# Second layer's mixer: PSUM banks split five and three instead of six and two

## The reference

```python
proj = xn @ cd_w_in[j]
lru_x, lru_g, m_x, m_o, m_if = split_cols(proj, CD_SIZES)      # 512, 512, 512, 512, 8
y_a = rglru_group(lru_x, lru_g, ...)   # recurrent unit
y_b = mlstm_group(m_x, m_o, m_if, ...) # four heads of 128
mixed = jnp.concatenate([y_a, y_b], axis=-1)
h = h + mixed @ w_mix_out[layer]
```

## Time and profile before

| | |
|---|---|
| median of 3 runs | 3127.95 us (3123.73 to 3131.43) |
| profiled execution | 3129.56 us, of which the span of the trace 3127.8 us |
| TensorE busy | 3019.6 us, 97% |
| VectorE, ScalarE, GpSimd busy | 1737.6, 1273.0, 319.1 us |
| mixer of the second layer | from 1049.7 us (first x matmul) to 1254 us (end of out7) |

### The profile page before, as it was taken

How to read it: one execution, slowest core, us unless ns; L and a number is a source line. 1 busy time by engine, 2 the same in 40 slices (tenths; PEclk the granted TensorE clock), 3 DMA queues, 4 the chain that set the end, 5 groups by cost and what they waited for, 6 DMA issues and landing times.

```text
span 3127.8 us, 41482 instructions
## 1 busy us (share of the span) xinstructions
PE 3019.6 (97%) x17696; PEld 2470.8 (79%) x17696; DVE 1737.6 (56%) x2154; ACT 1273.0 (41%) x1702; POOL 319.1 (10%) x285
## 2 busy tenths in 40 slices
PE   8989889999999999999999998999999999999999
PEld 5877778777888766777888775689998888878998
DVE  6444454646544675546544755676666453566665
ACT  5433333433322564433322545544444333344442
POOL 1010001000000100000000200124221000013240
PEclk9999999999999999999999999999999999999999
DMA  5341023223332311323332231233332223233331
GB/s 184 111 112 29 29 73 125 98 78 81 96 91 86 113 57 54 108 68 92 97 88 89 88 86 36 54 91 102 100 114 91 85 85 97 69 87 102 100 106 65
DMA packets 340104, 274.89 MB, mean 88 GB/s; under 512 B 28768, under 2 KB 308832, under 8 KB 339408
## 3 DMA queue, kind: packets, MB, share of 16 engines
q1 hardware_dynamic: 335552, 252.83, 27.2%
q0 software_dynamic: 4368, 19.41, 1.8%
HBM read 263.83 MB, written 8.39 MB: 87 GB/s over the span
## 4 chain that ended last, share of the span: by engine, by line
PE 86%; DVE 7%; ACT 5%; issue 1%; POOL 0%; DMA 0%; DVEq 0%; SPq 0%; ACTq 0%; POOLq 0%
PE ps L189 85%; ACT arena L203 2%; DVE arena L220 2%; ACT whi L206 2%; DVE arena L212 1%; DVE wlo L212 1%; PE ps L192 1%; DVE hT L212 1%; DVE xlo L212 0%; ACT L203 0%; POOL arena L212 0%; DVE sml L229 0%; ACT arena L206 0%; DVE xlo L220 0%; DVE split L212 0%
## 5 line engine op out<-in xcount | busy, mean ns | idle before, releaser
L189 PE MATMUL ps<-split,whi 128*128 128x512 f32 (+1 forms) x3008 | 900.9, 377 | 14.5 <-DVE split L212 6.1
L212 DVE TENSOR_TENSOR wlo<-wraw,whi 128x2048 fp32r<-128x2048 f32 (+5 forms) x261 | 562.3, 2157 | 486.1 <-ACT whi L206 485.8
L189 PE MATMUL ps<-xhi,whi 128*128 128x512 f32 (+2 forms) x2040 | 766.7, 381 | 25.5 <-DVE wlo L212 10.1
L189 PE MATMUL ps<-xhi,wlo 128*128 128x512 f32 (+2 forms) x1984 | 743.7, 375 | 0.0
L189 PE MATMUL ps<-xlo,whi 128*128 128x512 f32 (+2 forms) x1944 | 731.1, 376 | 0.0
L189 PEld LDWEIGHTS ps<-split,whi 128*128 128x128 f32 x3008 | 548.3, 188 | 142.7 <-issue 24.9
L206 ACT ACTIVATE whi<-wraw 128x2048 fp32r<-128x2048 f32 (+5 forms) x261 | 457.2, 1755 | 347.6 <-PE ps L189 243.3
L189 PE MATMUL ps<-split,wlo 128*128 128x512 f32 (+1 forms) x1504 | 559.1, 372 | 0.0
L189 PEld LDWEIGHTS ps<-xhi,whi 128*128 128x128 f32 (+1 forms) x2040 | 382.2, 189 | 109.9 <-issue 14.4
L189 PEld LDWEIGHTS ps<-xhi,wlo 128*128 128x128 f32 (+1 forms) x1984 | 374.9, 189 | 69.5 <-issue 5.1
L189 PEld LDWEIGHTS ps<-xlo,whi 128*128 128x128 f32 (+1 forms) x1944 | 366.7, 189 | 68.9
(11 more groups left out here) (132 smaller groups left out, 2428.2 us busy)
## 6 DMA issues: line engine op xcount, KB each, us to landing
wraw<-in_ffn_w_up SPq DMA_DIRECT2D x128, 512.0 KB, 5.2
wraw<-in_odd_w_in SPq DMA_DIRECT2D x24, 1024.0 KB, 5.1
wraw<-in_ffn_w_gate SPq DMA_DIRECT2D x44, 512.0 KB, 4.0
wraw<-in_ffn_w_down SPq DMA_DIRECT2D x20, 1024.0 KB, 5.1
wraw<-in_ffn_w_down SPq DMA_DIRECT2D x24, 768.0 KB, 4.5
wraw<-in_xattn_wkv SPq DMA_DIRECT2D x16, 1024.0 KB, 5.6
wraw<-in_xattn_wq SPq DMA_DIRECT2D x8, 1024.0 KB, 5.2
wraw<-in_xattn_wo SPq DMA_DIRECT2D x8, 1024.0 KB, 5.2
```

Source lines behind the costliest of these rows:

```text
L189: return self.e.matmul(out, lhsT, rhs, start=start, stop=stop, skip_group_check=True)
L212: return self.e.tensor_tensor(out, a, b, op)
```

## The change

The tuple for the heads and gates becomes five banks and the one for the dense blocks three:

```diff
@@ -2596,7 +2596,7 @@
             o_lru = add_units("lru_out", [P] * 4, Wo[0:512, :])
             o_ml = add_units("out", [P] * 4, Wo[512:1024, :])
-            of, of_dense = (0, 1, 2, 3, 4, 5), (6, 7)
+            of, of_dense = (0, 1, 2, 3, 4), (5, 6, 7)
 
             def tensor(pe):
```

## The result

The changed kernel takes 3142.3 us (median of 6 runs, 3136.11 to 3145.43) against 3127.37 us for the kernel before in the same runs: ratio 1.0043, 95% interval 1.0033 to 1.0053, that is 13.4 us more (10.3 to 16.6); the two medians by themselves differ by 14.9. The forecast was 10.9 us more, 3138.9, in a range of 3132 to 3146. So the direction and the range are right, and the median is 3.4 us above the forecast. The profiled execution took 3144.8 us, its span 3143.0.

The account below looks back on a forecast made before the run. TensorE, busy 97% of the span, was taken to bound the kernel. The terms 1.95 + 1.0 + 5.15 + 2.1 + 0 + 0.7 gave 10.9 us more, 3138.9 us from a median of 3127.95, range 3132 to 3146.

Parts of the forecast that it names:

- Step 1: At i2, which takes r0's bank: TensorE waits 1.95 us for r0's Sigmoid, and ScalarE's chain moves too.
- D: Delay of ScalarE's chain from i2's wait and the clock behind it: 3.0 us, between 1.95 and 3.65.
- The clock behind it: Behind i2's wait: work lost to a slow TensorE clock, 1.0 us taken between 0 and 1.7.
- Step 2: At g2: its 4.23 us wait and slow clock go, but s0 then waits for k0's copy.
- Step 3: At M1, which takes the bank of head 0's first scores: 5.15 us late, waiting for VectorE's weighing.
- The clock behind M1: Slow TensorE clock after the wait before M1: 2.1 us lost, between 1.7 and 3.4.
- Step 4: At M2, which takes the bank of s1's first scores: just free, 0 us, upper end 4.25.
- Step 5: At out 0, which takes sum 3's bank and waits for root 3: 0.7 us more.
- Rival (a): Faster: g2's wait and slow clock go and the time isn't given back, 3121.5 us; chance 0.05.
- rival (b): No clear change: waits as forecast, but the clock holds after both, 7.8 us, 3135.8; chance 0.17.

Follow-up runs that it names:

- m1_own: Changed kernel, but M1 on dense bank 5: ratio 1.0034 to the kernel before.
- m1m2_own: Changed kernel, but M1 on dense bank 5 and M2 on dense bank 6: ratio 1.0012 to the kernel before.
- hi_early: Changed kernel, but ScalarE rounds the weight unit of o0 and o1 right behind the Gelu of g0 and g1: ratio 1.0031 to the kernel before.
- silu_late: Changed kernel, but ScalarE does head 3's silu behind the copies of v2, v3, q0 and k0: ratio 1.0047 to the kernel before.
- phase: Changed kernel with the turn of the five banks moved on by one before sum3; one profiled execution, stage 214.43 us.
- all_own: Changed kernel, but i2 and M1 on dense bank 5 and M2 on dense bank 6: ratio 1.0006 to the kernel before.
- before_m1: Kernel before, six and two banks, but M1 on bank 4, the bank of s0.0: ratio 1.0033 to the kernel before.
- ahead_phase: The kernel ahead with the turn of the five banks moved on by one before sum3: ratio 0.9994 to the kernel before.
- ahead_again: The same kernel as ahead_phase, timed anew: ratio 0.9989 to the kernel before, 3123.5 us.
- i2_own: Changed kernel, but i2 on bank 5: ratio 1.0025 to the kernel before.
- ahead: Changed kernel with i2 on bank 5, M2 on bank 7, hi_early's rounding, g3 before s0, o0 before M1: ratio 0.9995 to the kernel before.

## Why the prediction was right, step by step

The mechanism was right, step by step, at i2, s0, M1, M2 and out0; the two terms for the clock were each off by 0.8 to 1 us, and that they cancel is luck.

- Step 1, i2: 1.95 us forecast; 1.83 us of idle time, M1 earlier by 2.1 from the stage's entry and the stage shorter by 2.6 when it is taken away. That ScalarE's chain moves by D was the step that carried all later ones, and it did, by 2.1 us.
- The clock behind it: 1.0 us taken between ends of 0 and 1.7; it was 0. The granted clock was 1.00 over 4.66 us, and the same wait of 1.8 us left the clock at 1.00 and the shift of the following blocks unchanged in m1_own, m1m2_own, hi_early, silu_late and phase too. D was therefore 2.1 us and not 3.0. The two cases that the term was taken from are not the only ones: in the kernel before there is also 1.94 us at 2743.76, with 0.69 over the 5.3 us behind it.
- Step 2, g2: the wait went and came back at s0, 4.19 us. Right. The clock behind it was 0.62 and cost nothing, since M1 waited anyway; in m1_own and all_own, where M1 had no wait behind it, it cost 1.8 and 2.8 us.
- Step 3, M1: 5.15 us forecast. Against before, M1 came 9.08 us later, of which 1.87 from before the stage and 2.1 from i2: 5.1. before_m1 shows it alone, 5.11.
- The clock behind M1: the mis-sized term. Forecast 2.1; from M1 to s1.0 the shift grew from 9.08 to 11.96, so 2.9. M1 itself ran slow, which I had not counted, and the half clock lasted longer than behind g2. The 2.9 lie inside the forecast's ends, 1.7 to 3.4. In the other kernels the same term was 1.6 to 3.1 us.
- Step 4, M2: 0 forecast with a margin under 1 us. No wait; the weighing ended 1163.31 and M2 started 1164.16, 0.85 us later. m1_own shows what stood behind the margin.
- Step 5, out0: 0.7 forecast, 0.76 measured (the shift grew from 11.96 to 12.72), 0.7 in phase.

Sum in the stage: 10.9 forecast, 10.85 measured. The agreement to 0.1 us is luck, since 1.0 us too much behind i2 meets 0.8 too little behind M1; the waits alone are right to about 0.1 us each. Of the 13.4 us of the timed runs 2.5 are then not in the stage; their interval reaches down to 10.3, and the profiled execution had 1.9 us more before the stage and 2.5 after it, at places where both kernels have the same instructions and banks. From the next stage's first matmul to the last matmul's end the profiled executions took 1865.0 to 1871.5 us over all kernels here. Much of this scatter can be seen where it arises: the same short waits behind the stage are followed by a low clock in one execution and not in the next. One such wait, 1.72 us in the kernel before and 1.73 in the changed one, and the clock behind it:

```profile
1979.67 0.50 PE L189 MATMUL ps<-split,whi 128*128 128x512 f32 x1 [1.72 <-DVE split L212]
1979.70:1984.36 4.66, 4.66 (x19) 2.75 (x20) 1.40 (x5) 1.16 (x3) 0.00 (x0) 1.00 0.01 4
...
1992.77 0.57 PE L189 MATMUL ps<-split,whi 128*128 128x512 f32 x1 [1.73 <-DVE split L212]
1992.80:1997.46 4.66, 4.66 (x12) 2.69 (x13) 1.40 (x5) 0.68 (x2) 0.00 (x0) 0.63 0.02 4
```

It costs 1.6 us in the second case. ahead_phase and ahead_again, one kernel, differ at the same place in the same way (0.63 and 1.00), and by 2.7 us over the whole part behind the stage. So the 2.5 us of the profiled execution need no effect of the change. In the timed runs, though, the difference from the kernel before lies above that of the stage in eleven of twelve comparisons, by up to 3.7 us (0.4 below it in i2_own), each with an interval of 3 to 4 us either way. Whether a part of that is an effect of the change on later stages stays open.

Rival (a), 3121.5, was wrong for this kernel, and rival (b) held behind i2 and failed behind M1 (clock 0.50). The Trainium skill (Perfetto Trace Analysis, Optimizing Tensor Performance, Matmuls) asks that independent groups rotate through different banks. The trace agrees for g2, whose wait of 4.2 us went; the rule says nothing of s0, which then waited as long for another reason.

## What to carry to other kernels

A bank taken out of a ring changes every group's predecessor, so list for each group who held the bank before and when that one is released; the loss sits where a group now follows one that is released late in another engine's own order (M1 behind a weighing). A wait removed from the full engine is won only up to the next thing it needs from the chain that feeds it, and a wait can hide the next one, so price the one behind it too. Here the time that an extra buffer freed was used only when work was moved into it (all_own against ahead), not by the buffer alone.

## What the runs showed of the hardware

The wait of 1.83 us at i2 never lowered TensorE's clock (six kernels), though one of 1.95 in the kernel before did, and one of 1.73 in the changed kernel. A short wait's effect is not fixed by its length: the wait of 1.95 us that stands at 1355.34 in the kernel before was followed by 0.63 over 4.66 us in eight of the fourteen profiled executions here and by 1.00 in six. Waits of 3.9 to 5.7 us at M1 or M2 halved the clock in all six kernels that have one (2.4 to 1.2 GHz, 0.50 over 4.4 us) and cost 2.3 to 3.1 us more than the wait; 2.7 us, in two kernels, cost 1.6. The wait of 4.2 us at s0 cost 1.8 us more in m1_own and 2.8 in all_own. In these cases a wait cost between 0.4 and 0.75 of its length again.
